# Hybrid retention and attention layer with experts: row copies of 64 partitions, an earlier transpose order, identity products in waits, experts' weights in 4 KB runs, early high parts

## What is computed

```
mod = silu(c) @ w_ada + b_ada                     # six vectors per stream
h   = rms_norm(x, g1) * (1 + sc1) + sh1
rq, rk, rv, rg, dq, dk, dv, gates = split(h @ w_in)
ret_o  = rms_norm(retention(rope(rq), rope(rk), rv, state)) * silu(rg)      # 4 heads
diff_o = rms_norm(diff_attention(...))                                      # 8 heads
x   = x + gt1 * ((sig(g_r) * (ret_o @ w_br_ret) + sig(g_d) * (diff_o @ w_br_diff)) @ w_out)
h2  = rms_norm(x, g2) * (1 + sc2) + sh2
x   = x + gt2 * sum_e combine[:, e] * ((silu(h2 @ w1[e]) * (h2 @ w3[e])) @ w2[e])   # top 2 of 16 experts
```

## Time and profile before

| what | value |
|---|---|
| median of 3 runs | 1566.76 us (1566.05 to 1568.14) |
| the profiled execution | 1567.25 us, span 1565.4 us |
| mean granted clock of PE | 0.973 |
| PE busy | 1466.7 us (94% of the span), 7676 products |
| PEld, DVE, ACT, POOL busy | 71%, 52%, 42%, 18% |
| moved by DMA | 302.89 MB, mean 193 GB/s; in the experts 386 to 394 |

### The profile page before, as it was taken

One profiled execution on the slowest core, in us unless ns is written; L12 is line 12 of the kernel. 1 busy time (PEld: TensorE's weight loads), 2 busy tenths in 40 slices (PEclk: granted clock), 3 DMA queues, 4 the chain that ended last, 5 costly groups with the idle time before them and its releaser, 6 DMA issues.

```text
span 1565.4 us, 21146 instructions
## 1 busy us (share of the span) xinstructions
PE 1466.7 (94%) x7676; PEld 1105.7 (71%) x7676; DVE 815.2 (52%) x1424; ACT 650.6 (42%) x1073; POOL 284.2 (18%) x174
## 2 busy tenths in 40 slices
PE   5999999999999999999999899999999799999991
PEld 3775777577757775777877676677787578877781
DVE  3332441253124312221866777644455899988995
ACT  5313311331223122313446445544223378888881
POOL 2342224223322331233000000000312100000002
PEclk9999999999999999999999999999998699999996
DMA  9565466446645664522441353245831799999996
GB/s 351 158 151 164 159 195 138 152 159 203 148 134 180 195 135 138 185 72 84 160 135 41 103 181 109 68 149 167 264 115 58 242 326 394 394 386 387 390 339 228
DMA packets 166427, 302.89 MB, mean 193 GB/s; under 512 B 16123, under 2 KB 43947, under 8 KB 166197
## 3 DMA queue, kind: packets, MB, share of 16 engines
q1 hardware_dynamic: 162582, 291.06, 56.9%
q0 software_dynamic: 3744, 10.49, 1.9%
HBM read 257.84 MB, written 46.81 MB: 195 GB/s over the span
## 4 chain that ended last, share of the span: by engine, by line
PE 35%; DMA 9%; DVE 5%; issue 2%; ACT 2%; POOL 0%; DVEq 0%; ACTq 0%; POOLq 0%; SPq 0%
PE pj L93 9%; PE pj L95 9%; PE pj L94 8%; DMA m_raw<-w 6%; PE d_B L2555 1%; DMA ring_raw<-w_out 1%; PE d_B L2574 1%; PE d_B L2582 1%; DMA d_kc<-cache_diff_k 1%; PE d_B L2616 1%; ACT m_hi L1450 1%; PE d_B L1628 1%; PE d_B L2564 1%; PE d_B L2543 1%; DVE m_oh L1535 1%
## 5 line engine op out<-in xcount | busy, mean ns | idle before, releaser
L93 PE MATMUL pj<-ring_hi,hT_hi 128*128 128x512 f32 x880 | 370.3, 421 | 7.9 <-DVE hT_lo L738 3.1
L95 PE MATMUL pj<-ring_hi,hT_lo 128*128 128x512 f32 x880 | 346.6, 394 | 0.0
L94 PE MATMUL pj<-ring_lo,hT_hi 128*128 128x512 f32 x880 | 346.0, 393 | 0.0
L513 POOL TENSOR_TENSOR ring_lo<-ring_raw,ring_hi 128x1024 fp32r<-128x1024 f32 x79 | 190.0, 2408 | 503.1 <-ACT ring_hi L587 502.9
L1532 DVE TENSOR_TENSOR m_lo<-m_raw,m_hi 128x1024 fp32r<-128x1024 f32 x188 | 224.5, 1223 | 25.2 <-ACT m_hi L1450 22.9
L587 ACT ACTIVATE ring_hi<-ring_raw 128x1024 fp32r<-128x1024 f32 x79 | 83.3, 1057 | 366.9 <-DMA ring_raw<-w_in 355.4
L1450 ACT ACTIVATE m_hi<-m_raw 128x1024 fp32r<-128x1024 f32 x188 | 195.1, 1059 | 30.8 <-DMA m_raw<-w 29.7
L93 PEld LDWEIGHTS pj<-ring_hi,hT_hi 128*128 128x128 f32 x880 | 167.3, 190 | 51.5 <-issue 17.9
L95 PEld LDWEIGHTS pj<-ring_hi,hT_lo 128*128 128x128 f32 x880 | 166.5, 189 | 37.0
L94 PEld LDWEIGHTS pj<-ring_lo,hT_hi 128*128 128x128 f32 x880 | 167.6, 190 | 28.5 <-issue 1.0
L785 DVE SCALAR_TENSOR_TENSOR r_S<-r_S,g,r_sm 128x512 f32<-128x512 f32 x64 | 45.0, 744 | 136.9 <-PE r_sm L1028 136.9
(11 more groups left out here) (357 smaller groups left out, 2301.7 us busy)
## 6 DMA issues: line engine op xcount, KB each, us to landing
m_raw<-w SPq DMA_DIRECT2D x188, 512.0 KB, 11.0
ring_raw<-w_in SPq DMA_DIRECT2D x72, 512.0 KB, 3.8
r_S<-state_ret SPq DMA_DIRECT2D x64, 256.0 KB, 4.7
r_ada_raw<-w_ada SPq DMA_DIRECT2D x16, 1024.0 KB, 6.8
o_state_s<-r_S SPq DMA_DIRECT2D x64, 256.0 KB, 4.5
a_raw<-w_ada SPq DMA_DIRECT2D x8, 1024.0 KB, 11.9
ring_raw<-w_in SPq DMA_DIRECT2D x32, 256.0 KB, 3.8
ring_raw<-w_br_ret SPq DMA_DIRECT2D x16, 512.0 KB, 4.0
```

The source lines that it names most:

```text
L93: pe.matmul(out, s_hi, m_hi, start=start, stop=False)
L94: pe.matmul(out, s_hi, m_lo, start=False, stop=False)
L95: return pe.matmul(out, s_lo, m_hi, start=False, stop=stop)
L513: pool.tensor_tensor(lo[:, p], raw[:, p], hi[:, p].bitcast(F32), ALU.subtract).then_inc(lo_done, 1)
```

## The change

Five edits. (1) The eight loads of a head's rows are one per column group a and half s, 64 partitions each, one row of 3 KB on each; the same bytes go to the same places. (2) At the start PE turns x for q = 0 to 7 ahead of the second piece of w_ada instead of q = 0 to 5, and transposes modulation piece 0 ahead of that too; ACT takes q = 8 and then makes the high part of QK0's first piece. (3) `stay_busy(n)` issues n products of the identity with itself (128x128, float32) into a PSUM bank that nobody reads, at places where PE waits. (4) w1 and w3 of the experts go to the partitions as "(r k)": partition r gets rows 256 p + 2r and 256 p + 2r + 1, one run of 4 KB, and the transposes of the gathered rows take every second column to match. (5) The high parts of the first expert's w1 are made one after each of the roots of tiles 0 to 3.

```diff
@@ -409,11 +409,10 @@
                 for q in range(4):
                     sp.dma_start(vk_home[q, :, 0:RDV], (v4_hi, v4_lo)[q // 2][:].bitcast(F32)).then_inc(vk_out, 16)
                 sp.wait_ge(vk_out, 128 * (h + 1))
-                for q in range(4):
-                    rows = vk_home[q, :, 0:RDV + RDK].rearrange("(s i l) c -> s l i c", s=2, i=4)
+                rows = vk_home[0:4, :, 0:RDV + RDK].rearrange("q (s i l) c -> i s q l c", s=2, i=4)
+                for a in range(4):
                     for s in range(2):
-                        p0 = 64 * s + DEC_L * q
-                        sp.dma_start(vk[p0:p0 + DEC_L].bitcast(F32), rows[s]).then_inc(vk_in, 16)
+                        sp.dma_start(vk[64 * s:64 * s + 64, a].bitcast(F32), rows[a, s]).then_inc(vk_in, 16)
 
             def load_tab(h):
                 if h:
@@ -618,12 +617,11 @@
                                ACT.Copy).then_inc(oT_hi_done, 1)
 
             take_mod(0)
-            for q in range(0, 6, 2):
+            for q in range(0, 8, 2):
                 take_xT(q)
+            take_mod(1)
+            take_xT(8)
             split_hi("QK0", 0)
-            take_mod(1)
-            for q in range(6, 2 * NT, 2):
-                take_xT(q)
             for k in range(4):
                 if k == 2:
                     split_hi("QK0", 1)
@@ -891,6 +889,12 @@
             last.then_inc(cT_done, 1)
             pe.wait_ge(cT_taken, 2)
 
+            def stay_busy(n):
+                for i in range(n):
+                    pe.matmul(pj[4][:, 0:P], K.ident[:], K.ident[:], start=True, stop=True)
+
+            stay_busy(36)
+
             def ada(i):
                 pe.wait_ge(a_in[i], 32)
                 if i >= 2:
@@ -1115,13 +1119,14 @@
                     steps(h, 6)
 
             ada(0)
-            for q in range(6):
+            for q in range(8):
                 turn_x(q)
+            turn_mod(0)
             ada(1)
-            turn_mod(0)
-            for q in range(6, 2 * NT):
+            for q in range(8, 2 * NT):
                 turn_x(q)
             turn_mod(1)
+            stay_busy(16)
             hT = (K.hT_hi, K.hT_lo)
             u = 0
             for h in range(RH + 1):
@@ -1341,7 +1346,7 @@
             e += w == "w1"
         if w == "w2":
             return self.io[w][0, e, p % 2 * 256:p % 2 * 256 + 256, p // 2 * W:(p // 2 + 1) * W].rearrange("(k r) n -> r k n", k=2)
-        return self.io[w][0, e, p * 256:(p + 1) * 256].rearrange("(k r) n -> r k n", k=2)
+        return self.io[w][0, e, p * 256:(p + 1) * 256].rearrange("(r k) n -> r k n", k=2)
 
     def slot(self, n):
         return (n - 4) % RING
@@ -1610,14 +1615,18 @@
                         last = pe.matmul(self.list_bank(e)[:, e:e + 1], self.oh[e][:, t], self.tok[:, t, c:c + 1], start=(t + c == 0), stop=(t + c == NT))
                 last.then_inc(self.slots_done, 1)
 
+            def stay_busy(n):
+                for i in range(n):
+                    pe.matmul(self.Y[1][:, 0:P], K.ident[:], K.ident[:], start=True, stop=True)
+
             def turn_x(e):
                 pe.wait_ge(*self.rows_in(r, e))
                 if e:
                     pe.wait_ge(self.t_lo, r * (2 * N_EXP) + 2 * e)
                 for k in range(2):
                     for a in range(4):
-                        c = (4 * k + a) * P
-                        last = pe.transpose(self.T[k][:, a * P:(a + 1) * P], self.xe[e % 2][:, c:c + P], K.ident[:])
+                        c = (4 * k + a) // 2 * 2 * P + a % 2
+                        last = pe.transpose(self.T[k][:, a * P:(a + 1) * P], self.xe[e % 2][:, c:c + 2 * P - 1:2], K.ident[:])
                     last.then_inc(self.t_done, 1)
 
             def turn_a(e):
@@ -1649,7 +1658,9 @@
 
             for e in range(EARLY):
                 slots(e)
+                stay_busy(2)
             turn_x(0)
+            stay_busy(5)
             pe.wait_ge(self.t_lo, r * (2 * N_EXP) + 2)
             for p in range(4):
                 if p == 2:
@@ -2200,10 +2211,9 @@
                 root_x(t)
                 if t >= 1:
                     take_h2(t - 1, 1)
-                if t == NP_T - 1:
-                    for p in range(4):
-                        act.wait_ge(moe.loaded0[p], 16)
-                        act.activation(moe.hi0[p][:], moe.raw0[p][:], ACT.Copy).then_inc(moe.hi0_done, 1)
+                if t < NP_T:
+                    act.wait_ge(moe.loaded0[t], 16)
+                    act.activation(moe.hi0[t][:], moe.raw0[t][:], ACT.Copy).then_inc(moe.hi0_done, 1)
             for a in range(2):
                 take_h2(NP_T, a)
             act.wait_ge(shifted, 1)
@@ -2709,6 +2719,10 @@
                     last = pe.transpose(out[:, c * P:(c + 1) * P], K.h2[:, t, (4 * a + c) * P:(4 * a + c + 1) * P], K.ident[:])
                 last.then_inc(h_turned, 1)
 
+            def stay_busy(n):
+                for i in range(n):
+                    pe.matmul(pj[3][:, 0:P], K.ident[:], K.ident[:], start=True, stop=True)
+
             def logits(t):
                 pe.wait_ge(h_taken, 2 * t + 2)
                 if t == 0:
@@ -2746,10 +2760,15 @@
                 if t + 2 < NT:
                     turn_merged(t + 2)
             turn_h2(3, 1)
+            pe.wait_ge(pj_free[3], LAST + 2)
+            stay_busy(8)
             logits(3)
+            stay_busy(4)
             for a in range(2):
                 turn_h2(4, a)
+            stay_busy(4)
             logits(4)
+            stay_busy(22)
             pe.wait_ge(assigned, 1)
             flat = lambda x: x.rearrange("p t e -> p (t e)")
             pe.matmul(B[0][:, 0:NE], tri[:, P:2 * P], Atot[:], start=True, stop=True).then_inc(total_done, 1)
```

## The result

**The changed kernel is slower: a median of 1581.84 us (1577.92 to 1584.73, 5 runs) against 1566.76 us, a ratio of 1.0091 with a 95% interval of 1.0075 to 1.0106.** 1548 us had been forecast, a gain of 1.2%; it lost 0.9%. The profiled execution took 1577.92 us, the shortest of the five; its span is 1576.1 us, 10.7 us more than before; its mean granted clock is 0.978. TensorE is busy for 1490.0 us in 7924 records, 23 us and 248 records more than before: these are the 124 identity products, two records each.

A forecast was written before the change was run, and what follows sets the result against it. TensorE, busy nearly throughout, was taken as the bound, its idle and lower-clock time the gain. 2.5 + 3.8 + 7.2 + 5.7 = 19.2 us off 1567.25 gave 1548 us; range 1541 to 1580, a fifth left out.

The forecast's parts named there:

- The row copies: Retention heads: copies into 64 partitions take about 7 us a head, ending TensorE's wait for copied rows; 3.8 us gained.
- The first rival: Row copies: outermost count 4 leaves 4 of 16 engines, so copies get slower; 1573 us in all, chance 0.34.
- The start: Start to chunk 0: full clock and added order, less a slowed DVE operation; 2.5 us gained, bounds 0.5 and 3.8.
- The added order: Start: eight transposes, chunk 0 of the modulation, then the second w_ada piece; keeps 1.2 us at DVE's first modulation.
- the collision: Start: GpSimd's low-part subtraction runs beside DVE's modulation and slows it; priced 0 to 2.1 us, taken as 1.1.
- The entry: Entry to the experts: five terms, a to e, with 0.3 us subtracted for products behind lists; 7.2 us gained, bounds 3 and 9.
- Term a: Entry: spread high parts keep GpSimd's low parts away from DVE's one-column operations of the last tile; 2.8 us gained.
- the terms b to e: Entry, full clock: last logits 1.7 us, counting products 0.7, first transposes 0.75, first expert products 1.5, less 0.3.
- The experts: Experts: 4 KB runs cut queue time, 18.45 to 17.8 us each over nine; 5.7 us gained, bounds 0 and 6.6.
- The other rivals: Fillers do little, DVE bounds the entry: 1557 us, chance 0.08; every-second-column reads double a transpose: 1562 us, chance 0.06.

The follow-up runs named there:

- e3: The changed kernel with the order of a half's copied rows turned round, so the source's outermost count is 16 instead of 4: 1547.54 us, ratio 0.9883.
- e2: The kernel before with the new row copies alone (64 partitions, outermost count 4): 1601.01 us, ratio 1.0230.
- e8: e3 with the start of before: old order of transposes, and no 36 and no 16 identity products there: 1549.68 us, ratio 0.9883.
- e7: e3 with the first expert's four high parts in a row after the root of tile 3, as before: 1549.66 us, ratio 0.9891.
- e5: e3 without the identity products at the entry to the experts and in the experts, and without their one wait: 1552.62 us, ratio 0.9907.
- e10: e3 with the gathered rows' transposes of neighbouring columns, 4 KB runs kept; another result, same amount of work: 1548.44 us.
- e9: e3 with QK0's first piece split ahead of DVE's modulation, and 12 identity products instead of 16 behind the modulation's transposes: 1545.60 us, ratio 0.9863.
- e11: e9 with one identity product instead of two behind each expert's list, and eleven in the second expert's 2.8 us wait: 1546.19 us, ratio 0.9876.
- e12: e3 once more, unchanged, run beside e11 on one chip: 1546.89 us, ratio 0.9884.

## Why the prediction was wrong

The forecast of all parts but one stood within the error of its terms, and that one had the other sign. The kernel was to get 1.2% faster and got 0.9% slower; its time, 1581.84 us, lies just above the range's upper end of 1580.

- **The row copies (forecast 3.8 us gained) is the step that failed.** "I take about 7, since a destination four times as wide removes what is special in today's copies" took the width for the only thing that changed. The outermost count fell from 16 to 4 in the same edit. The width was right (e3: no wait, 260 GB/s, 6.8 us a head), but the count decided first (e2: share 0.26): a head's copies took 18.2 us, not 7. Instead of 3.8 us gained the heads lost 27.7. With e3's order the edit is what the forecast described, and the time 1547.54 us for a forecast of 1548. That it comes so near is in part luck: by stage e3's profiled execution gains 5.4 us at the start and in the heads (6.3 forecast), 6.2 at the entry (7.2) and 5.3 in the experts (5.7), and another 3.1 in the stretch that no edit touches.
- **The first rival named the mechanism, with a smaller chance than the forecast and too small a price.** The argument against it, that the copies of before were slow with all queues busy, says what limited the old copies and nothing of the new. It priced 15.2 us of new waiting and 6 of clock. Measured: 24.9 - 3.8 = 21.1 of waiting and, since the heads end 25.8 us later with 1.9 gained at the start, 27.7 - 21.1 = 6.6 of clock. From the first issue to the first use a head took 14.93 us before and 20.16 after, 5.2 more where 3.8 was priced. The packets show where it went: a head's copies take 18.2 us instead of the 16.0 priced. From 108 to 113 us and from 116 to 119 us 32 to 35 of their packets begin in each us, from 113 to 116 and from 119 to 122 only 19 to 29, beside packets of the next weights; that these slow them, and what the longer issue adds (5.46 instead of 3.62 us), is argued, not shown. So 21.2 became 27.7. The other parts gained 13.2 where 15.4 was priced, and the untouched stretch another 3.8: 10.7 us more in the profiled execution, 1578 instead of 1573, and without that 3.8 it would have been 1582.
- **The start (2.5):** 1.9 by e8, and 1.9 in the changed kernel, whose copies are issued at 103.75 instead of 105.69. The full clock for the first piece of w_ada (1.92 us) and for chunk 0 came as written. The added order brought 1.5 instead of 1.2, and the collision that I had priced at 1.1 us out of 0 to 2.1 came at its upper bound, 2.0.
- **The entry (7.2):** 4.9 + 1.3 = 6.2 in the changed kernel. Term a (2.8) is 3.0 by e7; the terms b to e (4.35) are 3.6 by e5. The lists are part of what is missing: with two identity products behind each, TensorE sets their pace, every 0.78 us instead of 0.74, and from the first list to the first expert's transposes it takes 9.42 us instead of 8.70. That is 0.7 us, where 0.3 was put.
- **The experts (5.7):** 5.1 over twelve periods in the changed kernel, 5.6 in e3. The period is 17.80 us, as forecast, but not for the reason given: the queues were to set it, and in e3 TensorE does, by the stepped transposes, put at nothing, which cost 0.08 us above 17.72. Without them TensorE waits again in three of the periods (e10).
- **The other rivals.** The identity products did their work (e5), and a stepped transpose was not doubled (10 ns of TensorE's time each, where a doubling was 110).

## What to carry over

A DMA's pattern has two properties that an edit can change together: how many partitions it fills and how many engines its outermost count gives it. Write down both counts for both sides before pricing it, and if the consumer doesn't care for the order, put the dimension of 16 outermost. A queue share of a quarter at a fraction of the rate was here the sign of a copy on too few engines, a share of 1 at a low rate that of too narrow a destination. A step that is won on one engine may be lost by starting beside GpSimd; here moving the other party was enough (e9). And when a total agrees with the forecast, compare the stages: here 3.1 of the 20 us that e3's profiled execution gained came from work that no edit touches.

## What the runs showed that was not expected

- 260 GB/s into 64-partition destinations, at a share of 0.96; 125 into 16-partition ones at 1.05. A packet of 3 KB takes 182 ns into the first and 361 into the second, with about 14 under way in both.
- A weight load of every second column of float32 takes 209 ns instead of 141, nearly all hidden; and in e10, without it, twelve experts took as long as in e3, since TensorE then waited in three of them.
- The lower clock came at a stretch where TensorE counted as busy for 5.93 of 6 us, in short products (e11), and came or stayed away behind the same wait of 2.8 us in two executions of one kernel (e3, e12).
- The untouched stretch between the heads and the logits varied by 6.6 us among these kernels, which is more than any one of the four edits that gained is worth. It is TensorE's idle time and its time at the lower clock that vary, the rest is the same within 1.3 us; what moves these two stays open.
